# A two-layer hybrid decoder trunk on one core: buffers moved by 32 bytes, another place for one split block, and new orders at the ends of the output passes

## The chip, the cores and the metric

The kernel runs on one core of one Trainium2 chip. The metric is device time in microseconds (us) of that core, lower is better. The span of a profile runs from the first to the last instruction.

## The reference, cut to what matters

x is (1024 positions, 1024 channels), all float32. Each of two layers computes

```
h = rmsnorm(x) * (1 + scale) + shift          # scale, shift, gate from c_act @ mod_w[layer]
layer 0: proj = h @ hy_w_in   (1024 x 6144)    # six parts of 8 heads, 128 channels each
         ya = rg_lru(conv4(xa)) * silu(ga);  yb = gb_post * conv3(gc_pre * v) * silu(gb)
layer 1: proj = h @ pool_w_in (1024 x 4096)    # values v and gates g
         y = ((window_mean(v) - v) @ w_grp + b) * scale * silu(g)      # four groups of 512
x = x + gate * (y @ w_out)                     # w_out is 2048 x 1024
```

and the result is one more rmsnorm of x, times `final_g`.

## The kernel before, in words

**Precision.** Every large product is made of float32 operands split into an upper part (fp32r, by ScalarE) and a remainder (VectorE), and three matmuls: upper*upper, upper*lower, lower*upper (L2113, L2114, L2115 in `products`). Most are 128 x 128 weights against 512 columns.

**Order.** Every engine has its program written out by hand, with semaphores between them. Layer 0 goes head by head (Strassen-like pairs of products for heads 1 to 7), and spills each head's two blocks of y to DRAM. Then come the *passes*: pass A of layer 0 makes output blocks 0 to 2 (128 positions each), B makes 3 to 5, C makes 6 and 7; pass A of layer 1 makes 0 to 3 and B makes 4 to 7. A pass has 16 steps, one for each block of 128 channels of y. A step needs its rows of `w_out` (`split_hi` L865 on ScalarE, `split_lo` L1369 on VectorE) and its block of y (`split_y`, L932 and L1436). Three steps are held at a time, so both splits of step n wait until TensorE has counted step n-3 done (`o_step`, set at the last block's second half). A block has two halves of 512 columns, each with a bank of PSUM. All but the last `LAST` steps (2, in pass B of layer 1 it is 3) go step by step through the pass's blocks; the last ones go block by block: for each block, for each of these steps, both halves (L2462 to L2467). So blocks are complete one after the other.

**y's places.** The split y blocks of layer 0 lie in a ring of three: `y_at_r` over head buffer 0, `y_at_aux` over `aux`, and `y_at_xc` over head buffer 2 (XC, later SIGB), which is read last by `gate_b(7)` (L1675). In layer 1 they lie inside X. X, `w_hi`, `w_lo` and `raw` stand ahead of the small vectors in SBUF, all head buffers, the pooled differences `d_hi` and `d_lo` and layer 0's y behind them and behind `pad_small`, of 32 bytes. X begins at byte 640 of its partition and `w_hi` at byte 115,328, multiples of 64; the head buffers begin at 163,488, and everything behind them at an offset from there that is a multiple of 64 (`d_hi` at 180,128).

**After a block.** `residual` (L1811, L1815) multiplies each half by the gate and adds it to the rows of x. `squares` (L1167, L1170) makes the sum of squares of the row and its root, `inverse` (L1821) the reciprocal. In layer 0, `normalize` (L1175) scales the row, and TensorE transposes it back (`turn`, L2248: three groups of eight, woven behind steps by the table BEHIND, L147 to L150), ScalarE modulates (`modulate`, L1184 to L1194) and VectorE takes the lower part (`low_h1`). In layer 1, `row_out` (L1826) scales the row by its inverse and `final`, and SyncE stores it (`store`, L682).

**Ends.** After pass C, VectorE splits V0 and V1, does `low_h1(1, 7)`, and then `gate_of_layer_1` (L1842), which TensorE waits for before it goes on. At the kernel's end VectorE does, for each of blocks 4 to 7, `residual(1, b)` and `row_out(b)` (L2105 to L2107).

Of the kernel before, what the change touches and what calls it, by code (L numbers as in the profile page):

```python
# [109 lines left out]
def build(nc, x, c, norm_g, mod_w, mod_b, hy_w_in, hy_conv_w, hy_conv_b, lru_w_a, lru_b_a, lru_w_x, lru_b_x,  # L110
# [36 lines left out]
    BEHIND = {(0, "B", 5): ["mod1"], (0, "C", 13): ["gate1"]}  # L147
    for k in range(KB):
        BEHIND.setdefault((0, "B", 6 + k), []).append(("T", 0, k))
        BEHIND.setdefault((0, "C", 5 + k), []).append(("T", 1, k))  # L150

    def outputs(layer, p):

# [66 lines left out]
    with ExitStack() as ctx:  # L220
        def sb(name, shape, dt=F32, stack=ctx):
            return stack.enter_context(nc.sbuf_tensor(name, shape, dt))

        def sem(name):
            return ctx.enter_context(nc.semaphore(name))
# [24 lines left out]
        pos = sb("pos", [P, PAD], mybir.dt.int32)  # L250
        icnt = sb("icnt", [P, GROUPS, PAD])
        fix = sb("fix", [P, PAD])
        sb("pad_small", [P, PAD // 2])


        with ExitStack() as phase:
# [19 lines left out]
        with ExitStack() as phase:  # L276
            y_at_r = sb("y_at_r", [P, S], F32R, phase)
            sb("pad_r", [P, S], F32, phase)
            y_at_xc = sb("y_at_xc", [P, S], F32R, phase)
            xc_hi_ = sb("xc_hi_", [P, S], F32R, phase)  # L280
            xc_lo_ = sb("xc_lo_", [P, S], F32R, phase)
            sb("pad_heads", [P, 9, S], F32, phase)
            y_at_aux = sb("y_at_aux", [P, S], F32R, phase)
        with ExitStack() as phase:
            sb("pad_pool", [P, 4, PAD + S], F32, phase)
# [5 lines left out]
        def halves(ap):  # L291
            return ap.rearrange("p (a b) -> p a b", a=2)
# [45 lines left out]

        def y_half(n, which):

            return halves((y_at_r, y_at_aux, y_at_xc)[n][:, :])[:, which, :]


        def piece(at, width, dt=F32):
# [122 lines left out]
        mixed_done = sem("mixed_done")  # L467
        pads = sem("pads")
        row_ready = sem("row_ready")

        def v(name, n=0, count=1):
            return vec[:, COL[name] + n:COL[name] + n + count]
# [80 lines left out]
        def _(sp):  # L553
# [228 lines left out]
            for n, step in enumerate(s for s in STEPS if s[0] == 1):  # L782
# [11 lines left out]
                    sp.dma_start(final, final_g.rearrange("(a n) -> a n", a=1).broadcast_to([P, D])).then_inc(gate_in, 16)  # L794
                if p == "B" and at in (5, 7, 9, 11):
                    store((at - 5) // 2)
            for b in range(4, SB):
                store(b)
            sp.wait_ge(out_done, 16 * SB)

        LAM_STEPS = 3
        CONSTS = 6
# [55 lines left out]
        def _(act):  # L858
# [58 lines left out]
            def take_21(q):  # L917
                act.wait_ge(full_of["4"], q + 1)
                nc.scalar.activation(dst(q)[1][:, S1], bank(q, "a"), ACT.Copy, scale=-1.0).then_inc(neg21, 1)
# [234 lines left out]
                prep(cc, 6)  # L1154
            split_hi(("W", 0, "A", TIME_ORDER[1]))
            take_21(Q["C", HEADS - 1])
            sigmoid_b(HEADS - 1)
            split_hi(("W", 0, "A", TIME_ORDER[2]))
            act.wait_ge(sgb_done, HEADS)
            split_y((0, "A", TIME_ORDER[2]))  # L1160


            def squares(layer, b):
# [33 lines left out]
            def passes(layer, begin):  # L1197
                for n, step in enumerate(s for s in STEPS if s[0] == layer):
                    if n < begin:
                        continue  # L1200
                    p, at = "ABC"[n // 16], n % 16
                    step_splits(step)
                    if (p, at) == ("A", 15):
                        load_root()
                    if layer == 0:
                        if p == "B" and at in (2, 3, 4):
                            squares(0, at - 2)
                        if p == "B" and at in (3, 4, 5):
                            normalize(at - 3)
                        if p == "B" and at >= 9:  # L1210
                            modulate(0, at - 9)
                        if (p, at) == ("C", 0):
                            modulate(0, 7)
                        if p == "C" and at in (3, 4, 5):
                            squares(0, at)
                        if p == "C" and at in (4, 5, 6):
                            normalize(at - 1)
                        if p == "C" and at >= 8:
                            modulate(1, at - 8)
                    elif p == "B" and at in (3, 4, 5, 6):  # L1220
                        squares(1, at - 3)

# [127 lines left out]
            step_splits(first[1])  # L1350

            passes(1, 2)
            for b in range(4, SB):
                squares(1, b)

        @block.vector
        def _(dve):
# [315 lines left out]
            def gate_b(i):  # L1673
                dve.wait_ge(sgb_ready, i + 1)
                nc.vector.tensor_tensor(SGB, SGB, SIGB if i else area(("gb", 0)), ALU.mult).then_inc(sgb_done, 1)  # L1675
# [103 lines left out]
                inputs_of_scan(i)  # L1779
            recur(HEADS - 1)  # L1780
            split_lo(("W",) + first[1])
            gate_b(HEADS - 1)
            out_a(HEADS - 1)
            step_splits(first[2])
            out_b(HEADS - 1)


# [35 lines left out]
            def row_out(b):  # L1823
                inverse(1, b)
                dve.wait_ge(rstd_ready, SB + b + 1)
                nc.vector.scalar_tensor_tensor(out=XN[1][b], in0=XR[1][b], scalar=rstd[:, 2, b:b + 1], in1=final,  # L1826
                                               op0=ALU.mult, op1=ALU.mult).then_inc(row_ready, 1)

            def modulation_1():
                dve.wait_ge(*full("mod1"))  # L1830
# [30 lines left out]
            def passes(layer, begin):  # L1861
                for n, y_step in enumerate(s for s in STEPS if s[0] == layer):
                    p, at = "ABC"[n // 16], n % 16
                    if n >= begin:
                        if layer == 0 and p == "B":
                            if at == 1:
                                residual(0, 0)
                                residual(0, 1)
                            if at == 2:
                                residual(0, 2)  # L1870
                        if layer == 0 and p == "C":
                            if at == 1:
                                residual(0, 3)
                                residual(0, 4)
                            if at == 2:
                                residual(0, 5)
                        if layer == 1 and p == "B":
                            if at == 1:
                                residual(1, 0)
                                residual(1, 1)  # L1880
                                residual(1, 2)
                            if at == 2:
                                residual(1, 3)
                        step_splits(y_step)
                    if layer == 0:
                        for m in MODS_AT.get(n, ()):
                            add_mod(mods1[m])
                        if p == "B" and at in (2, 3, 4):
                            inverse(0, at - 2)
                        if (p, at) == ("B", 8):  # L1890
                            modulation_1()
                        if p == "B" and at >= 10:
                            low_h1(0, at - 10)
                        if p == "C" and at < 2:
                            low_h1(0, at + 6)
                        if p == "C" and at in (3, 4, 5):
                            inverse(0, at)
                        if (p, at) == ("C", 7):
                            window_counts()
                        if p == "C" and at >= 9:  # L1900
                            low_h1(1, at - 9)
                    elif p == "B" and at in (4, 5, 6, 7):
                        row_out(at - 4)

            passes(0, 3)
            split_lo(("V0", 0))
            split_lo(("V1", 0))
            low_h1(1, KB - 1)
            gate_of_layer_1()
            residual(0, 6)  # L1910
            inverse(0, 6)
# [190 lines left out]
            mixed(n, 3)  # L2102

            passes(1, 2)
            for b in range(4, SB):  # L2105
                residual(1, b)
                row_out(b)  # L2107

        @block.tensor
        def _(pe):  # L2110
# [340 lines left out]
            for layer, p in BLOCKS:  # L2451
                y_steps, blocks = [s for s in STEPS if s[:2] == (layer, p)], BLOCKS[layer, p]
                ends = 2 * KB - LAST[layer, p]
                for n, y_step in enumerate(y_steps[:ends]):
                    operands(y_step)
                    for b in blocks:
                        for half in range(2):
                            if (layer, p, n, b, half) == (0, "A", 0, 2, 1):
                                last_of(Q["C", HEADS - 1])
                            part_of(y_step, b, half)  # L2460
                    behind(layer, p, n)
                for b in blocks:  # L2462
                    for y_step in y_steps[ends:]:
                        if b == blocks[0]:
                            operands(y_step)
                        for half in range(2):
                            part_of(y_step, b, half)  # L2467
                for n in range(ends, 2 * KB):
                    behind(layer, p, n)
                if (layer, p) == (0, "C"):  # L2470
                    groups()
# [22 lines left out]
```

## Time and profile before

| | |
|---|---|
| three runs | 1337.77, 1338.64, 1338.72 us; median 1338.64 |
| the profiled execution | 1339.64 us, its span 1337.9 us |
| PE (matmul) | 1292.0 us busy, 97%, 5671 instructions |
| DVE (VectorE) | 936.2 us, 70%, 1122 |
| ACT (ScalarE) | 629.3 us, 47%, 885 |
| POOL | 271.4 us, 20%, 158 |
| granted TensorE clock | 0.982 of full speed |
| HBM read, written | 145.33 MB, 25.17 MB |

The profiled execution is 1.00 us above the median. Matmuls overlap their neighbours, so a row's duration (0.39 us) is longer than the distance from one start to the next; the distance is what counts. "[2.30 <-DVE ...]" behind a row is the engine's idle time before it and what ended it.

### The profile page before, as it was taken

The numbers are of one execution on the slowest core, as the hardware profiler recorded it, in microseconds if no ns is written. First come the engines' busy times: TensorE is split into PE (matmuls) and PEld (weight loads), VectorE is DVE, ScalarE is ACT, GpSimd is POOL, SyncE is SP. The second block draws the span as 40 slices with busy tenths as digits, with TensorE's granted clock in tenths as the row PEclk, the third lists the DMA queues.
The fourth block names the chain that finished last, engine by engine and source line by source line (L and its number), as shares of the span: only waits on it lengthen the run. The fifth ranks groups of instructions, "written<-read, shape, count | busy, mean of one in ns | idle before, by whom it ended". The sixth has DMA issues, their size and how long they took to land.

```text
span 1337.9 us, 15397 instructions
## 1 busy us (share of the span) xinstructions
PE 1292.0 (97%) x5671; PEld 1057.4 (79%) x5671; DVE 936.2 (70%) x1122; ACT 629.3 (47%) x885; POOL 271.4 (20%) x158
## 2 busy tenths in 40 slices
PE   4999999999999999999999999999999999999995
PEld 4877788888888888788877777888888888888884
DVE  6889887978878886767466597758658656435635
ACT  6465556564646465445467464243243143223422
POOL 0034433433534432000000022133133131000000
PEclk7899999999999999999899999999999999999998
DMA  9612241323232342597666202321320321873531
GB/s 297 196 49 67 63 130 55 123 83 110 67 110 85 93 130 79 198 380 266 231 200 221 79 16 64 101 88 32 110 79 33 110 79 41 300 247 128 215 108 63
DMA packets 145474, 171.51 MB, mean 128 GB/s; under 512 B 6582, under 2 KB 117366, under 8 KB 145400
## 3 DMA queue, kind: packets, MB, share of 16 engines
q1 hardware_dynamic: 145400, 170.53, 39.5%
q8 instruction: 46, 0.75, 0.2%
q14 instruction: 28, 0.23, 0.1%
HBM read 145.33 MB, written 25.17 MB: 127 GB/s over the span
## 4 chain that ended last, share of the span: by engine, by line
PE 82%; DVE 12%; issue 2%; ACT 2%; DMA 1%; SPq 0%; DVEq 0%; ACTq 0%
PE psum L2113 27%; PE psum L2115 27%; PE psum L2114 27%; DVE w_lo L1369 1%; DVE X L1459 1%; DVE win L1951 1%; DVE whole_x L1811 1%; DVE w_lo L1391 1%; DMA whole_x<-in_x 1%; DVE w_lo L1383 1%; DVE X L1465 1%; PE psum L2248 0%; ACT w_hi L865 0%; DVE d_lo L1969 0%; DMA raw<-in_hy_w_out 0%
## 5 line engine op out<-in xcount | busy, mean ns | idle before, releaser
L2113 PE MATMUL psum<-X,w_hi 128*128 128x512 f32 x1140 | 448.9, 394 | 9.9 <-DVE late L1842 2.8
L2115 PE MATMUL psum<-X,w_lo 128*128 128x512 f32 x1140 | 446.4, 392 | 0.0
L2114 PE MATMUL psum<-X,w_hi 128*128 128x512 f32 x1140 | 446.0, 391 | 0.0
L2113 PEld LDWEIGHTS psum<-X,w_hi 128*128 128x128 f32 x1140 | 215.5, 189 | 60.3 <-issue 9.1
L2115 PEld LDWEIGHTS psum<-X,w_lo 128*128 128x128 f32 x1140 | 215.2, 189 | 45.5
L2114 PEld LDWEIGHTS psum<-X,w_hi 128*128 128x128 f32 x1140 | 215.5, 189 | 44.7 <-issue 0.2
L1369 DVE TENSOR_TENSOR w_lo<-raw,w_hi 128x1024 fp32r<-128x1024 f32 x98 | 120.9, 1235 | 166.1 <-ACT w_hi L865 165.8
L865 ACT ACTIVATE w_hi<-raw 128x1024 fp32r<-128x1024 f32 x98 | 103.6, 1058 | 211.6 <-PE psum L2115 171.9
L887 ACT ACTIVATE w_hi<-ssum 128x512 fp32r<-128x512 f32 x140 | 87.2, 626 | 121.0 <-PE psum L2115 95.4
L1391 DVE TENSOR_TENSOR w_lo<-ssum,w_hi 128x512 fp32r<-128x512 f32 x140 | 119.1, 857 | 27.4 <-ACT w_hi L887 26.7
L826 POOL TENSOR_TENSOR ssum<-raw 128x512 f32<-128x512 f32 x35 | 62.0, 1772 | 302.4 <-DMA raw<-in_pool_w_in 266.2
L834 POOL TENSOR_TENSOR ssum<-ssum,raw 128x512 f32<-128x512 f32 x35 | 55.8, 1593 | 323.7 <-DVE w_lo L1391 323.7
L2113 PE MATMUL psum<-w_hi,X 128*128 128x512 f32 x256 | 99.8, 390 | 0.4 <-DVE X L1436 0.4
L2115 PE MATMUL psum<-w_hi,X 128*128 128x512 f32 x256 | 99.6, 389 | 0.0
L2114 PE MATMUL psum<-w_lo,X 128*128 128x512 f32 x256 | 99.6, 389 | 0.0
L837 POOL TENSOR_TENSOR ssum<-raw 128x512 f32<-128x512 f32 x35 | 78.2, 2234 | 73.4 <-DVE w_lo L1391 73.4
L831 POOL TENSOR_TENSOR ssum<-ssum,raw 128x512 f32<-128x512 f32 x35 | 61.5, 1759 | 49.3 <-DVE w_lo L1391 47.3
L1383 DVE TENSOR_TENSOR w_lo<-raw,w_hi 128x1024 fp32r<-128x1024 f32 x35 | 42.7, 1221 | 27.1 <-ACT w_hi L876 26.9
L2113 PEld LDWEIGHTS psum<-w_hi,X 128*128 128x128 f32 x256 | 48.0, 188 | 11.0 <-DVE w_lo L1369 0.8
L2115 PEld LDWEIGHTS psum<-w_hi,X 128*128 128x128 f32 x256 | 48.0, 188 | 10.1
L2114 PEld LDWEIGHTS psum<-w_lo,X 128*128 128x128 f32 x256 | 48.1, 188 | 9.9
L2113 PE MATMUL psum<-d_hi,w_hi 128*128 128x512 f32 x128 | 50.7, 396 | 0.3 <-DVE w_lo L1369 0.3
(239 smaller groups left out, 1959.4 us busy)
## 6 DMA issues: line engine op xcount, KB each, us to landing
raw<-in_hy_w_in SPq DMA_DIRECT2D x48, 512.0 KB, 5.1
raw<-in_hy_w_out SPq DMA_DIRECT2D x48, 512.0 KB, 4.7
raw<-in_pool_w_in SPq DMA_DIRECT2D x32, 512.0 KB, 5.2
raw<-in_pool_w_out SPq DMA_DIRECT2D x32, 512.0 KB, 3.6
aux<-in_mod_w SPq DMA_DIRECT2D x16, 512.0 KB, 4.2
y_dram<-bufs SPq DMA_DIRECT2D x16, 512.0 KB, 2.9
raw<-in_mod_w SPq DMA_DIRECT2D x16, 512.0 KB, 5.6
y_dram<-gb_ SPq DMA_DIRECT2D x16, 512.0 KB, 3.1
```

Source lines behind the costliest of these rows:

```text
L826: nc.gpsimd.tensor_tensor(even, a21, a22, ALU.add).then_inc(s_ready, 1)
L831: nc.gpsimd.tensor_tensor(odd, even, a11, ALU.add).then_inc(s_ready, 1)
L834: nc.gpsimd.tensor_tensor(even, odd, a12, ALU.add).then_inc(s_ready, 1)
L837: nc.gpsimd.tensor_tensor(odd, a21, a11, ALU.add).then_inc(s_ready, 1)
L865: nc.scalar.activation(flat(w_hi[:, es:es + 2, :]), raw[:, at, :], ACT.Copy).then_inc(hi_done, 1)
L887: nc.scalar.activation(w_hi[:, es, :], ssum[:, op % 2, :], ACT.Copy).then_inc(hi_done, 1)
L1369: nc.vector.tensor_tensor(flat(w_lo[:, es:es + 2, :]), raw[:, at, :], flat(w_hi[:, es:es + 2, :]).bitcast(F32), ALU.subtract).then_inc(lo_ ...
L1383: ins = nc.vector.tensor_tensor(w_lo[:, es:es + 2, :].rearrange("p two (k n) -> p two k n", k=KP), raw_blocks(q, 0), w_hi[:, es:es + 2, :] ...
L1391: ins = nc.vector.tensor_tensor(w_lo[:, es, :], ssum[:, op % 2, :], w_hi[:, es, :].bitcast(F32), ALU.subtract)
L2113: nc.tensor.matmul(out_, whi, xhi, start=first, stop=False, skip_group_check=check)
L2114: nc.tensor.matmul(out_, whi, xlo, start=False, stop=False, skip_group_check=check)
L2115: return nc.tensor.matmul(out_, wlo, xhi, start=False, stop=last, skip_group_check=check)
```

## The change

Five things. (1) `pad_small` goes, so all buffers behind it begin 32 bytes lower (the head buffers at 163,456). (2) The third place of y's ring lies over head buffer 8 (GBP) instead of buffer 2; GBP is last read by `gated_sc(7)`. The splits of step 2 of pass A move ahead of `sigmoid_b(7)` on ScalarE and ahead of `gate_b(7)` on VectorE, where `out_a(7)` moves ahead too. (3) The last steps of each pass go half by half: block, then half, then step. (4) The second group of transposes goes behind steps 4 to 11 of pass C instead of 5 to 12, with `modulate` and `low_h1` a step earlier. (5) At the end, VectorE does `residual(1, b+1)` ahead of `row_out(b)`; the last block has its squares, its scaled row and its store in halves.

```diff
-        BEHIND.setdefault((0, "C", 5 + k), []).append(("T", 1, k))
+        BEHIND.setdefault((0, "C", 4 + k), []).append(("T", 1, k))
...
-        sb("pad_small", [P, PAD // 2])
...
-            y_at_xc = sb("y_at_xc", [P, S], F32R, phase)
+            sb("pad_xc", [P, S], F32, phase)
...
+            y_at_gbp = sb("y_at_gbp", [P, S], F32R, phase)
...
-            for b in range(4, SB):
+            for b in range(4, SB - 1):
                 store(b)
-            sp.wait_ge(out_done, 16 * SB)
+            for half, cols in enumerate(HALVES):
+                sp.wait_ge(row_ready, SB + half)
+                sp.dma_start(out[0, (SB - 1) * P:SB * P, cols], XN[1][SB - 1][:, cols]).then_inc(out_done, 16)
+            sp.wait_ge(out_done, 16 * (SB + 1))
...  (ScalarE)
+            act.wait_ge(scg_done, HEADS)
+            split_y((0, "A", TIME_ORDER[2]))
+            split_hi(("W", 0, "A", TIME_ORDER[2]))
             sigmoid_b(HEADS - 1)
-            split_hi(("W", 0, "A", TIME_ORDER[2]))
-            act.wait_ge(sgb_done, HEADS)
-            split_y((0, "A", TIME_ORDER[2]))
...
-                        if p == "C" and at >= 8:
-                            modulate(1, at - 8)
+                        if p == "C" and 7 <= at < 15:
+                            modulate(1, at - 7)
...
+            b = SB - 1
+            for half, cols in enumerate(HALVES):
+                act.wait_ge(o_evac, o_count(1, b, half))
+                nc.scalar.activation(XN[1][b][:, cols], XR[1][b][:, cols], ACT.Square,
+                                     accum_out=ss[:, 2 * half, b:b + 1]).then_inc(sq_done, 1)
+                act.wait_ge(sq_done, 2 * SB + half)
+                if half == 0:
+                    nc.scalar.activation(ss[:, 1, b:b + 1], ss[:, 0, b:b + 1], ACT.Identity, scale=1.0 / D,
+                                         bias=cst[:, 0:1]).then_inc(half_done, 1)
+                    act.wait_ge(half_done, 1)
+                else:
+                    nc.scalar.activation(sd[:, 2, b:b + 1], ss[:, 2, b:b + 1], ACT.Sqrt, scale=1.0 / D,
+                                         bias=ss[:, 1, b:b + 1]).then_inc(root_done, 1)
...  (VectorE)
+            out_a(HEADS - 1)
+            split_y(first[2])
+            split_lo(("W",) + first[2])
             gate_b(HEADS - 1)
-            out_a(HEADS - 1)
-            step_splits(first[2])
             out_b(HEADS - 1)
...
-                        if p == "C" and at >= 9:
-                            low_h1(1, at - 9)
+                        if p == "C" and at >= 8:
+                            low_h1(1, at - 8)
...
-            low_h1(1, KB - 1)
             gate_of_layer_1()
...
-            for b in range(4, SB):
-                residual(1, b)
-                row_out(b)
+            residual(1, 4)
+            residual(1, 5)
+            row_out(4)
+            residual(1, 6)
+            row_out(5)
+            residual(1, 7)
+            row_out(6)
+            last_row_out()     # inverse, then the scaled row in two halves, row_ready after each
...  (TensorE)
                 for b in blocks:
-                    for y_step in y_steps[ends:]:
-                        if b == blocks[0]:
-                            operands(y_step)
-                        for half in range(2):
+                    for half in range(2):
+                        for y_step in y_steps[ends:]:
+                            if (b, half) == (blocks[0], 0):
+                                operands(y_step)
                             part_of(y_step, b, half)
```

## Rows read from the trace of the kernel before

**Rows 1.** The page's chain that ended last, by engine.
```profile
PE 82%; DVE 12%; issue 2%; ACT 2%; DMA 1%; SPq 0%; DVEq 0%; ACTq 0%
```
**Rows 2.** Timeline, PE, layer 0 pass A: start us, us; 53 distances between these.
```profile
582.09 0.40 PE L2113 MATMUL psum<-w_hi,y_at_r 128*128 128x512 f32 x1
...
594.46 0.40 PE L2115 MATMUL psum<-w_hi,y_at_xc 128*128 128x512 f32 x1
```
**Rows 3.** Timeline, PE, layer 1 pass A into B: 402 distances between these.
```profile
1150.49 0.40 PE L2113 MATMUL psum<-w_hi,X 128*128 128x512 f32 x1
...
1241.63 0.45 PE L2113 MATMUL psum<-w_hi,X 128*128 128x512 f32 x1
```
**Rows 4.** Timeline, PE, mixing of group 0: 71 distances between these.
```profile
854.02 0.40 PE L2113 MATMUL psum<-d_hi,w_hi 128*128 128x512 f32 x1
...
870.59 0.40 PE L2115 MATMUL psum<-d_hi,w_lo 128*128 128x512 f32 x1
```
**Rows 5.** Timeline, PE, a gate product of six matmuls, then the next product.
```profile
209.38 0.39 PE L2113 MATMUL psum<-xc_hi_,g_hi 128*128 128x512 f32 x1
...
210.76 0.39 PE L2113 MATMUL psum<-X,w_hi 128*128 128x512 f32 x1
```
**Rows 6.** Groups by form, ACT, squares: name, count | busy, mean ns | idle.
```profile
L1167 ACT ACTIVATE whole_x<-whole_x 128x1024 f32<-128x1024 f32 x8 | 8.4, 1053 | 17.9 <-DVE whole_x L1815 17.9
L1167 ACT ACTIVATE whole_x<-bufs 128x1024 f32<-128x1024 f32 x8 | 8.4, 1049 | 7.2 <-DVE bufs L1815 7.2
```
**Rows 7.** Timeline, the start of layer 0's pass A.
```profile
544.75 0.60 ACT L919 ACTIVATE bufs<-psum 128x512 f32<-128x512 f32 x1 [5.66 <-PE psum L2115]
...
547.79 1.23 DVE L1675 TENSOR_TENSOR bufs<-bufs 128x1024 f32<-128x1024 f32 x1 [3.47 <-ACT bufs L1064]
...
551.90 0.47 PE L2113 MATMUL psum<-w_hi,y_at_xc 128*128 128x512 f32 x1 [2.30 <-DVE y_at_xc L1436]
...
552.92 0.33 SPq L635 DMA_DIRECT2D y_dram<-bufs  x1
...
561.01 0.47 PE L2113 MATMUL psum<-w_hi,y_at_aux 128*128 128x512 f32 x1 [0.47 <-DVE y_at_aux L1436]
```
**Rows 8.** Timeline, layer 0, pass B's end and pass C's first steps.
```profile
686.91 1.06 ACT L865 ACTIVATE w_hi<-raw 128x1024 fp32r<-128x1024 f32 x1 [4.83 <-PE psum L2115]
...
694.31 0.48 PE L2113 MATMUL psum<-w_hi,y_at_aux 128*128 128x512 f32 x1 [0.49 <-DVE y_at_aux L1436]
...
702.51 1.14 ACT L1175 ACTIVATE whole_x<-bufs,rstd 128x1024 f32<-128x1024 f32 x1
...
705.60 0.49 PE L2248 MATMUL psum<-ident,whole_x 128*128 128x128 f32 x3
```
**Rows 9.** Timeline, the end of pass C and the first matmul behind it.
```profile
736.78 1.06 ACT L865 ACTIVATE w_hi<-raw 128x1024 fp32r<-128x1024 f32 x1 [4.85 <-PE psum L2115]
...
740.87 0.50 PE L2113 MATMUL psum<-X,w_hi 128*128 128x512 f32 x1 [2.79 <-DVE late L1842]
```
**Rows 10.** Timeline, ACT, layer 1, the split for step 1 of pass B.
```profile
1235.77 1.06 ACT L865 ACTIVATE w_hi<-raw 128x1024 fp32r<-128x1024 f32 x1 [7.94 <-PE psum L2115]
```
**Rows 11.** Timeline, layer 1, the last splits and blocks of pass B.
```profile
1307.95 1.06 ACT L865 ACTIVATE w_hi<-raw 128x1024 fp32r<-128x1024 f32 x1 [3.86 <-PE psum L2115]
...
1311.02 0.47 PE L2113 MATMUL psum<-w_hi,X 128*128 128x512 f32 x1 [0.45 <-DVE X L1436]
...
1329.04 0.68 DVE L1811 TENSOR_TENSOR whole_x<-psum,whole_x 128x512 f32<-128x512 f32 x1
...
1331.82 1.06 ACT L1167 ACTIVATE whole_x<-whole_x 128x1024 f32<-128x1024 f32 x1 [4.20 <-DVE whole_x L1815]
...
1333.52 1.28 DVE L1826 SCALAR_TENSOR_TENSOR whole_x<-whole_x,rstd 128x1024 f32<-128x1024 f32 x1
```
**Rows 12.** DMA view of 1300 to 1338 us: GB/s in 40 slices of 0.95 us.
```profile
GB/s 0 0 0 0 0 0 0 0 0 9 0 0 0 0 0 0 0 0 0 177 358 17 17 0 0 177 375 0 0 0 0 190 362 0 0 0 0 198 354 0
```
**Rows 13.** Windows: length, PE, PEld, DVE, ACT, POOL busy (count), PEclk, DMA share, GB/s.
```profile
740.00:744.00 4.00, 3.13 (x8) 2.47 (x9) 3.41 (x6) 0.49 (x1) 0.00 (x0) 0.67 0.00 1
```

More of the change, by code:

```diff
@@ L278, in build @@
             sb("pad_r", [P, S], F32, phase)
-            y_at_xc = sb("y_at_xc", [P, S], F32R, phase)
+            sb("pad_xc", [P, S], F32, phase)
             xc_hi_ = sb("xc_hi_", [P, S], F32R, phase)
             xc_lo_ = sb("xc_lo_", [P, S], F32R, phase)
-            sb("pad_heads", [P, 9, S], F32, phase)
+            sb("pad_heads", [P, 3, S], F32, phase)
+            y_at_gbp = sb("y_at_gbp", [P, S], F32R, phase)
+            sb("pad_late", [P, 5, S], F32, phase)
             y_at_aux = sb("y_at_aux", [P, S], F32R, phase)
@@ L339, in y_half @@
         def y_half(n, which):
-            return halves((y_at_r, y_at_aux, y_at_xc)[n][:, :])[:, which, :]
+            return halves((y_at_r, y_at_aux, y_at_gbp)[n][:, :])[:, which, :]
         def piece(at, width, dt=F32):
@@ L469, in build @@
         row_ready = sem("row_ready")
+        half_done = sem("half_done")
         def v(name, n=0, count=1):
@@ L1352, in _ @@
             passes(1, 2)
-            for b in range(4, SB):
+            for b in range(4, SB - 1):
                 squares(1, b)
+            b = SB - 1
[11 more added lines that the diff above has]
+                                         bias=ss[:, 1, b:b + 1]).then_inc(root_done, 1)
         @block.vector
@@ L1827, in row_out, with last_row_out @@
                                                op0=ALU.mult, op1=ALU.mult).then_inc(row_ready, 1)
+            def last_row_out():
+                b = SB - 1
+                inverse(1, b)
+                dve.wait_ge(rstd_ready, 2 * SB)
+                for cols in HALVES:
+                    nc.vector.scalar_tensor_tensor(out=XN[1][b][:, cols], in0=XR[1][b][:, cols],
+                                                   scalar=rstd[:, 2, b:b + 1], in1=final[:, cols],
+                                                   op0=ALU.mult, op1=ALU.mult).then_inc(row_ready, 1)
             def modulation_1():
@@ L2104, in _ @@
             passes(1, 2)
-            for b in range(4, SB):
-                residual(1, b)
-                row_out(b)
+            residual(1, 4)
[6 more added lines that the diff above has]
+            last_row_out()
         @block.tensor
```

## The prediction

> **What bounds the kernel now.** I read the chain that ended last first: TensorE is 82% of it, VectorE 12% [rows 1]. So a change pays where it shortens TensorE's row of matmuls, takes away a wait in it, or shortens what stands behind its last matmul. Next I read the distance between matmul starts in undisturbed stretches, since almost the whole span is such distances. Layer 1's y products take (1241.63 - 1150.49) / 402 = 226.7 ns each [rows 3]; layer 0's, the same instruction with its weights in the head buffers, 12.37 / 53 = 233.4 ns [rows 2]; mixing, where the columns streamed (d_hi) lie there, 16.57 / 71 = 233.4 ns [rows 4]. A gate product, both of whose operands lie there, takes 1.38 / 6 = 230 ns [rows 5]. Third come the waits: 2.30 and 0.47 us at steps 2 and 4 of pass A [rows 7], 0.49 at step 2 of pass C [rows 8], 2.79 at the end of pass C [rows 9], 0.45 in the last pass [rows 11]. Last comes the tail: matmuls end near 1324.7, the span at 1337.9.
>
> **Part 1, the start of buffers.** What the slow stretches share is an operand at 32 past a multiple of 64 bytes. The extra 6.6 ns is the same whether the weights (512 bytes a partition) or the columns (2048 bytes) begin there, as one more read of a 64-byte piece per operand would give: 16 float32 elements against 512 in 213 ns is 6.7 ns. I take 226.7 for all of them; bounds are 233.4 (no effect) and 226.7. Matmuls touched: 3 x 256 = 768 of layer 0's y, 4 x 96 = 384 of mixing, 96 of the gates at 3 ns. Whole: 768 x 6.6 = 5.1, 384 x 6.6 = 2.5, 0.3: 7.9 us. ScalarE's squares take 1053 ns in X and 1049 in the head buffers [rows 6], so I count nothing for the other engines and DMAs (bounds 0 to 1 us of gain).
> Not all of it arrives. Where a VectorE or ScalarE chain sets when TensorE may go on, its matmuls ahead are covered: 72 between step 13 of pass A and step 2 of B, and about 60 at B's end and C's start. Arriving: 0.3 and 0.1 ahead of the waits, pass A steps 4 to 13 180 x 6.6 = 1.2, B 252 x 6.6 = 1.6, C 129 x 6.6 = 0.85, mixing 2.5: **6.6 us**.
> On this the Trainium skill (SBUF — State Buffer, the table of properties) says that SBUF has cachelines of 16 bytes. A start at 32 past 64 is a whole line then, and by that rule the term would be 0. The trace's 233.4 against 226.7 speaks for a coarser piece.
>
> **Part 2, the third place of y.** Now sigmoid_b, gate_b (547.79), out_a and two splits stand ahead of 551.90 [rows 7]. In the new order y's upper part follows the copy at 544.75, so from 545.4; w's upper part to 546.8, w's lower to 548.1, ahead of the 549.4 at which TensorE asks: the 2.3 us go. Then the next thing is late. Behind the split stand a table load (1.28) and the sigmoid to 549.2, gate_b, out_b to 551.6; the last spill, now at 552.92, goes at 551.6, 1.3 earlier, and the loads for step 4 are queued behind it on SyncE. So step 4 starts at about 559.7 in place of 561.01, with a wait of some 2 us ahead of it: **1.3 us** gained of 2.8. If the DMA queues, busy from there on, set the pace alone, it is 0; if they carry the earlier start fully, 2.3.
>
> **Part 3, half by half.** The step before the last is now counted done 3 matmuls (0.7 us) before the pass's end, not 6, so the first split for the next pass starts 0.7 later.
> - A to B: VectorE is in residuals until 612.6 and hides it. 0.
> - B to C: ScalarE's split moves from 686.91 [rows 8] 0.7 later against TensorE, VectorE's chain behind it (w, y, low_h1, four residual operations, w, y) has no gap, and step 2 waits **0.7** longer.
> - C to layer 1: VectorE's chain from ScalarE's 736.78 to 740.87 [rows 9] starts 0.7 later and loses low_h1(1, 7), 0.53: **-0.15**.
> - Pass A to B of layer 1: the chain from 1235.77 [rows 10] ends in residual(1, 3), whose second half frees the bank that 1241.63 [rows 3] just waited for: **-0.4**.
> - Last pass: three steps at the end. The third's operands are asked for after 6 matmuls, not 12, but come no sooner (released at 1307.95, ready at 1311.02 [rows 11]). The wait grows by 6 x 0.227 = 1.36 and TensorE ends 1.36 later. In the tail's sum below.
>
> **Part 4, transposes a step earlier.** The first now stands behind step 4 of C, whose end falls near 702.8; it needs normalize(5), which is ScalarE's 702.51 to 703.65 [rows 8], in a queue without a gap since 691. With step 2 later, TensorE waits some **0.5** more here (bounds 0, if ScalarE's queue slides ahead, and 1.0). B to C and this cost 1.2 together.
>
> **Part 5, the tail.** Now each of the last blocks costs VectorE a round trip: residual 1329.04 to squares 1331.82 (2.78), to the scaled row 1333.52 (1.70), row end 1334.80 [rows 11], 5.7 us a block against TensorE's 4.08 (18 x 0.227). Turned round, with the same durations: TensorE starts the third step's first half at 1311.02, block 7's halves are full at 1324.25 and 1326.3. VectorE takes them at 1325.0 and 1326.3 and ends 1327.7; first half's squares on ScalarE end 1327.1, the second's run 1327.7 to 1328.5, root 1328.8. VectorE meanwhile writes row 6 (to 1329.1), then the reciprocal and two half rows to 1329.9 and 1330.5, in place of 1334.80. Then 1 MB is under way at once: at 198 to 375 GB/s a slice [rows 12] 512 KB takes some 1.45 us, so from 1329.9 the three stores run to 1332.8, plus the 0.85 that the last slice lies ahead of the end now: 1333.7 against 1337.9, **4.2 us** gained. Bounds: 2.5 (half rows of 2 KB store more slowly), 4.8 (the last store lands unqueued).
>
> **Sum.** 6.6 + 1.3 - 1.2 - 0.15 - 0.4 + 4.2 = 10.3 us. Against the profiled execution's 1339.64 that is 1329.3; the median of the runs shown lies 1.0 lower, so **1328.3**.
>
> **Rivals.**
> - *The start does not matter, only the region* (0.10). For it: all slow operands lie behind byte 163,000, and the 16-byte lines of the skill's SBUF page would have it so. Against: with both operands there the distance is 230, not more. It gives 10.3 - 6.6 = 3.7 gained: 1334.9.
> - *The granted clock falls at a longer wait* (0.12). Behind the wait of 2.79 the clock was 0.67 of full over 4 us, 1.2 GHz for a part, and PE did 8 matmuls in place of 17 or so [rows 13]; behind the one of 2.30 it did not fall. New waits of about 2 us stand ahead of step 4 of A, in C and in the last pass. Price about 2 us each where nothing hides it: 1330.3 to 1332.3.
> - *The end is set by stores* (0.05). Two half stores and row 6 share the queues and the halves land late: tail gain 1.5 at most, 1331.0.
> - *Slower: the ring of transposes* (0.03). A transpose waits for modulate two before it, which is in ScalarE's queue behind a split that waits for TensorE. If the shift closes this ring, each of 8 steps of C grows. It decides from 1.3 us a step, 10.4 in all: 1339 or more. Against: before and after, each stands the same distance in steps from the other, and no such wait shows now.
> - That the change doesn't do what it says is not open for places and orders; for the pace it is the first rival.
>
> **Numbers.** The forecast itself has 0.66, with its own range 1326.0 to 1330.8 (the bounds of parts 2, 4 and 5); 0.04 is left for more gain than that, from DMAs or waits that shorten by themselves. 8 in 10: 1325.5 to 1333.0, which takes in the clock and the stores, and leaves out the first rival and the slower one. A measurement of this kernel can tell about 0.2%, 2.7 us, from nothing. Faster by more 0.91 (the first rival is 3.7 faster), within 0.05, slower 0.04.
>
> **What the profile after would show.** Distances of 226.7 ns between matmuls with y_at_* and d_hi; 233 would make the forecast wrong by 6 us. No wait at y_at_gbp's first use, one of about 2 us at step 4 of pass A. Longer waits at step 2 of C and at its first transpose. About 1.8 us of wait in the last pass, the last matmul 1.4 later against step 12, the last half row some 4 us after the last matmul's end, and the span's end 3 us behind that. A PEclk below 1.00 near 557, 694 or 1311 would be the second rival.

## The result, and the profile after

The changed kernel takes 1327.18 us in the median of five runs (1323.81 to 1330.55), the kernel before 1337.77 beside it (1336.99 to 1338.72). The ratio is 0.9923, with a 95% interval of 0.9902 to 0.9945. The prediction was 1328.3 us. The profiled execution took 1326.77 us, its span 1325.0, which is 12.9 us below the span before; the medians lie 10.6 us apart. All ratios are of fast executions: one of steps_back's six runs took 3335.56 us, nothing is known of why, and its ratio leaves that run out.

The page after, first its busy time, then the chain that ended last:

```profile
PE 1281.4 (97%) x5671; PEld 1054.8 (80%) x5671; DVE 936.2 (71%) x1123; ACT 629.6 (48%) x888; POOL 271.3 (20%) x158
...
PE 81%; DVE 13%; issue 2%; ACT 2%; DMA 1%; SPq 0%; DVEq 0%; ACTq 0%
```

The picture is that of [rows 1]: TensorE's row of matmuls sets the end. The same number of matmuls is 10.6 us less busy (1292.0 before).

The pace, that is the distance from one matmul's start to the next, by TensorE's timeline: 109 undisturbed distances between layer 0's y matmuls, then 71 in mixing.

```profile
575.07 0.39 PE L2147 MATMUL psum<-w_lo,y_at_gbp 128*128 128x512 f32 x1
...
599.77 0.39 PE L2148 MATMUL psum<-w_hi,y_at_gbp 128*128 128x512 f32 x1
...
847.63 0.39 PE L2146 MATMUL psum<-d_hi,w_hi 128*128 128x512 f32 x1
...
863.72 0.39 PE L2148 MATMUL psum<-d_hi,w_lo 128*128 128x512 f32 x1
```

24.70 / 109 = 226.6 ns where [rows 2] had 233.4, and 16.09 / 71 = 226.6 where [rows 4] had 233.4. Over all such distances y's mean is 227.5 to 227.7 (233.3 before), a gate product's 226.7 (229.9 before).

TensorE's waits, by its timeline, in brackets with the releaser:

```profile
555.68 0.47 PE L2146 MATMUL psum<-w_hi,y_at_aux 128*128 128x512 f32 x1 [2.01 <-DVE y_at_aux L1455]
...
687.65 0.47 PE L2146 MATMUL psum<-w_hi,y_at_aux 128*128 128x512 f32 x1 [1.37 <-DVE y_at_aux L1455]
...
696.88 0.55 PE L2281 MATMUL psum<-ident,whole_x 128*128 128x128 f32 x3 [0.78 <-ACT whole_x L1180]
...
734.66 0.58 PE L2146 MATMUL psum<-X,w_hi 128*128 128x512 f32 x1 [2.97 <-DVE late L1871]
...
1233.07 0.50 PE L2146 MATMUL psum<-w_hi,X 128*128 128x512 f32 x1 [0.29 <-DVE whole_x L1835]
...
1302.51 0.47 PE L2146 MATMUL psum<-w_hi,X 128*128 128x512 f32 x1 [1.80 <-DVE X L1455]
```

Step 2 of pass A waits no more. Step 4 waits 2.01 (0.47 in [rows 7]), step 2 of C 1.37 (0.49 in [rows 8]), the first transpose 0.78 (none), the end of C 2.97 (2.79 in [rows 9]), the last pass 1.80 (0.45 in [rows 11]).

The tail, VectorE's and TensorE's timeline, which answers to [rows 11]:

```profile
1316.40 0.68 DVE L1831 TENSOR_TENSOR whole_x<-psum,whole_x 128x512 f32<-128x512 f32 x1
...
1317.33 0.39 PE L2148 MATMUL psum<-w_hi,X 128*128 128x512 f32 x1
...
1319.28 1.28 DVE L1846 SCALAR_TENSOR_TENSOR whole_x<-whole_x,rstd 128x1024 f32<-128x1024 f32 x1
1320.48 0.15 DVE L1841 RECIPROCAL rstd<-sd 128x1 f32<-128x1 f32 x1
1320.67 1.42 DVE L1854 SCALAR_TENSOR_TENSOR whole_x<-whole_x,rstd 128x512 f32<-128x512 f32 x2
```

Block 7's residual begins ahead of the last matmul's start, at 1316.40; it began 4.5 us behind it before (1329.04 against 1324.51). The half rows end at 1322.1, the span 2.9 us later. From the last matmul's start to the end are 7.67 us, 13.39 before.

**How traces are compared below.** Some stretches run at half the clock, 1.2 GHz, and they differ between executions of one kernel. A product's matmul takes 0.427 us there instead of 0.227, so I count those at a distance of 0.36 to 0.45 us and take 0.2 us off for each (one or two in a profile can be counted wrongly): "row less clock" is the start of the last matmul, less the start of the first product near 35 us, less 0.2 us for each product's matmul at half clock. It leaves out what half clock costs the small matmuls. The most of that lies in layer 0's 32 column sums near 635 us, so the table has the time that these take, too.

| kernel | first product | last matmul | at half clock | row less clock | column sums | last matmul to end |
|---|---|---|---|---|---|---|
| before | 35.83 | 1324.51 | 38 | 1281.1 | 4.74 | 13.39 |
| tail_only | 34.38 | 1322.52 | 42 | 1279.7 | 3.63 | 8.28 |
| place_only | 35.70 | 1323.38 | 45 | 1278.7 | 3.63 | 13.32 |
| start_only | 35.88 | 1313.69 | 24 | 1273.0 | 3.63 | 13.31 |
| heads_256 | 35.72 | 1314.96 | 30 | 1273.2 | 3.63 | 13.34 |
| start_64 | 35.69 | 1319.83 | 29 | 1278.3 | 3.63 | 13.37 |
| heads_128 | 34.61 | 1319.19 | 35 | 1277.6 | 4.77 | 13.31 |
| changed kernel | 35.18 | 1317.33 | 26 | 1277.0 | 4.66 | 7.67 |
| after_again (same) | 35.68 | 1321.93 | 46 | 1277.1 | 3.96 | 7.67 |
| turns_back | 35.84 | 1319.83 | 40 | 1276.0 | 4.62 | 7.67 |
| steps_back | 35.83 | 1314.70 | 21 | 1274.7 | 4.43 | 8.30 |
| steps_again (same) | 35.38 | 1313.97 | 24 | 1273.8 | 4.13 | 8.33 |
| both_back | 34.66 | 1315.40 | 40 | 1272.7 | 3.83 | 8.30 |
| late_half | 35.30 | 1313.44 | 19 | 1274.3 | 4.48 | 7.66 |

Equal rows of matmuls agree in row less clock to 0.1 us (changed kernel and after_again), 0.9 (steps_back and steps_again) and 1.4 (before and tail_only). Of the 1.4, the column sums are 1.11. Their row in before's timeline of TensorE, then the windows of before and of tail_only around it (columns as in [rows 13]):

```profile
636.71 4.74 PE L2254 MATMUL psum<-ones,bufs 128*128 128x1 f32 x32
```

```profile
636.00:648.00 12.00, 12.00 (x58) 10.48 (x57) 3.98 (x7) 3.04 (x5) 0.00 (x0) 0.72 0.85 304
```

```profile
636.00:648.00 12.00, 12.00 (x65) 10.28 (x64) 4.61 (x7) 4.98 (x8) 0.00 (x0) 0.86 0.92 338
```

The granted clock was 0.72 of full speed there in before and 0.86 in tail_only. So kernels with equal column sums are compared best. What is smaller than that is read from single waits, which agree to some 0.02 us where the releaser is a chain of VectorE's.

### The profile page after: what moved, and what is told of

Its sections match the earlier page's. It is cut to its first block, busy times and chain, and to the rows that moved or that the text cites. A ratio compares the mean times of both kernels' runs of the same rounds, so it can differ in the third digit from the quotient of the medians.

```text
span 1325.0 us, 15403 instructions
## 1 busy us (share of the span) xinstructions
PE 1281.4 (97%) x5671; PEld 1054.8 (80%) x5671; DVE 936.2 (71%) x1123; ACT 629.6 (48%) x888; POOL 271.3 (20%) x158
## 4 chain that ended last, share of the span: by engine, by line
PE 81%; DVE 13%; issue 2%; ACT 2%; DMA 1%; SPq 0%; DVEq 0%; ACTq 0%
PE psum L2146 27%; PE psum L2147 26%; PE psum L2148 26%; DVE w_lo L1388 1%; DVE X L1478 1%; DVE win L1979 1%; ACT w_hi L870 1%; DVE whole_x L1831 1%; DVE w_lo L1410 1%; DMA whole_x<-in_x 1%; PE psum L2281 1%; DVE w_lo L1402 1%; DVE X L1484 1%; DVE d_lo L1997 0%; DVE macc L1503 0%
```

## The experiments

**One part alone.** Three kernels put one part of the change into the kernel before.

start_only, the start of the buffers:

```
-        sb("pad_small", [P, PAD // 2])
```

> Nothing but the start of the buffers changes. Theory of the prediction (an operand that begins 32 bytes past a multiple of 64 costs each matmul 6.6 ns): layer 0's y matmuls 226.7 to 227.7 ns apart in place of 233.4, mixing 226.7, gate products 226.7 in place of 230; the waits at steps 2 and 4 of pass A, at step 2 of C and at the end of C as before; 6.6 us less than before, 1331.2. Rival (only the region counts, not the start): 233.4 ns as before, the time within 1 us of before's. If the scanning and splitting engines also gain: more than 7.9 us less.

Measured: 1328.37 us, ratio 0.9940 (0.9925 to 0.9955), 8.0 us of 1337.1. TensorE's timeline of start_only, 109 distances in layer 0 and 71 in mixing:

```profile
572.01 0.39 PE L2113 MATMUL psum<-w_lo,y_at_aux 128*128 128x512 f32 x1
...
596.71 0.39 PE L2114 MATMUL psum<-w_hi,y_at_aux 128*128 128x512 f32 x1
...
845.86 0.39 PE L2112 MATMUL psum<-d_hi,w_hi 128*128 128x512 f32 x1
...
861.95 0.39 PE L2114 MATMUL psum<-d_hi,w_lo 128*128 128x512 f32 x1
```

24.70 / 109 and 16.09 / 71 are 226.6 ns; y's mean is 227.5 to 227.7, gate products 226.7. The waits at step 2 of pass A (2.44) and at the end of C (2.83) are nearly as before. The others are not, against the expectation: step 2 of C waits 0.78 in place of 0.49, a wait of 0.28 is new at step 2 of B, and step 4 of pass A doesn't wait, as six matmuls ran at half clock ahead of it. Row less clock is 1273.0; tail_only, whose column sums took the same 3.63 us and whose row of matmuls is before's, has 1279.7: 6.7 us. The forecast had 6.6 arriving of 7.9; the interval of the runs, 6.0 to 10.0 us, holds both. The pace rests on the start, and the first rival falls.

tail_only, the order behind the last pass (residuals ahead of rows, halves for the last block):

> Before with nothing but the order behind the last pass: residuals ahead of the scaled rows, the last block's squares, scaled row and store by halves. The matmuls keep their old order, so TensorE ends as before and the last block's first half is full only 0.7 us ahead of its end. My theory (VectorE's round trips set the end): the last half row some 4 us after the last matmul, the stores 3 us more, 5.5 us less than before: 1332.3. Rival (stores set the end): half rows land late, at most 3 us less, 1334.8 or more. In either case nothing changes ahead of 1311 us.

Measured: 1332.85 us, ratio 0.9960 (0.9945 to 0.9976). The last matmul to the end takes 8.28 in place of 13.39: 5.1 us, near my 5.5 and not the rival's 3. By the ratio of the runs it is 5.3 us (3.2 to 7.4).

place_only, y's third place and the orders it allows:

> Before with nothing but y's third buffer in another place and the orders that this allows. My theory: the wait of 2.30 us at step 2 of pass A goes, and one of about 2 us stands at step 4 (0.47 before), as the loads behind the last spill come no more than 1.3 us earlier: 1.3 us less than before, 1336.5. Rival 1 (the loads carry it fully): 2.3 less and 0.5 us of wait at step 4. Rival 2 (DMA queues pace it): 0 less, a wait of 2.8 at step 4; a clock below full behind it would add 1 to 2 us.

Measured: 1335.78 us, ratio 0.9989 (0.9978 to 1.0000), so 1.5 us with 0 in its interval: the runs alone can't tell it from nothing. TensorE's timeline of place_only, step 4 of pass A:

```profile
559.69 0.47 PE L2116 MATMUL psum<-w_hi,y_at_aux 128*128 128x512 f32 x1 [1.87 <-DVE y_at_aux L1438]
```

No wait at step 2, and 1.87 at step 4, which starts at 559.69 against the 561.01 of [rows 7]: 1.3 us, as forecast. Eight matmuls behind this wait ran at half clock, so its 1.3 could be lost again in this execution.

**Where a buffer should begin.** The start alone tells that 32 bytes matter, not which piece. start_64 makes the gap 64 bytes in place of 32 (PAD is 16 elements of 4 bytes):

```
-        sb("pad_small", [P, PAD // 2])
+        sb("pad_small", [P, PAD])
```

> Before with the 32 bytes ahead of the big buffers made 64: they begin at an odd multiple of 64 bytes, where in the changed kernel they begin at a multiple of 512. If the piece that an operand should begin with is 64 bytes, the same as with the start alone: 226.7 ns and 6.6 us less, 1331.2. If it is 128 bytes or more, 233.4 ns and before's time, 1337.8.

Measured: 1336.31 us, ratio 0.9991 (0.9983 to 0.9999). TensorE's timeline of start_64, 54 distances in layer 0 and 71 in mixing:

```profile
583.24 0.39 PE L2113 MATMUL psum<-w_hi,y_at_r 128*128 128x512 f32 x1
...
595.84 0.39 PE L2113 MATMUL psum<-w_hi,y_at_r 128*128 128x512 f32 x1
...
850.76 0.40 PE L2113 MATMUL psum<-d_hi,w_hi 128*128 128x512 f32 x1
...
867.03 0.39 PE L2115 MATMUL psum<-d_hi,w_lo 128*128 128x512 f32 x1
```

12.60 / 54 = 233.3 ns for y, as slow as with 32 bytes, and 16.27 / 71 = 229.2 for mixing, between the two paces. So the piece is not 64 bytes. A gap of 128 bytes ahead of the whole region (start_128) gave no time: SBUF has 16,352 bytes a partition left for a buffer of 16,384. The next two start from start_only and move only the buffers in the heads' region, y's among them, by 128 and by 256 bytes; mixing's stay:

```
+            sb("pad_bufs", [P, 32], F32, phase)      # 64 in heads_256
             bufs = sb("bufs", [P, 12, S], F32, phase)
...  (the same ahead of xT and of y_at_r, which begin at the same byte)
```

> The kernel with the start alone, and 128 bytes ahead of y's buffers and of those that share their place (mixing's stay where they are, at 256 past a multiple of 512). With y 32 or 64 bytes past a multiple of 128 its matmuls stood 233.4 ns apart, at a multiple of 512 they stand 227.6. If the piece is 128 bytes: 227.6 here. If it is 256 or 512 bytes: 233.4. Mixing 226.7 in either case.

> As the kernel with y's buffers 128 bytes further, but 256 bytes: y begins at 256 past a multiple of 512, as mixing's streamed columns do in the kernel with the start alone, which stand 226.7 ns apart. If the piece that matters is 256 bytes: y's matmuls 227.6 ns apart and the time of the kernel with the start alone, 1328.4. If it is 512 bytes for the weights: 233.4 ns and 1334 as with 128 bytes. If y is slow from the shift of its neighbours and not from its own start: 233.4 ns too, at 128 and at 256 alike.

heads_128 took 1334.31 us (one run, so it has no interval), heads_256 1330.11, ratio 0.9952 (0.9936 to 0.9969). TensorE's timeline of heads_128, 106 distances in layer 0, and of heads_256, 109:

```profile
575.20 0.39 PE L2116 MATMUL psum<-w_lo,y_at_aux 128*128 128x512 f32 x1
...
599.83 0.39 PE L2117 MATMUL psum<-w_hi,y_at_aux 128*128 128x512 f32 x1
```

```profile
575.22 0.39 PE L2116 MATMUL psum<-w_lo,y_at_aux 128*128 128x512 f32 x1
...
599.93 0.39 PE L2117 MATMUL psum<-w_hi,y_at_aux 128*128 128x512 f32 x1
```

24.63 / 106 = 232.4 ns and 24.71 / 109 = 226.7. heads_128's pace is that of the expectation's case of 256 or 512 bytes, but for 1 ns, and heads_256 decides for 256. The expectations count the starts from X and leave out the 640 bytes ahead of it. By true byte addresses, modulo 256 (X and `w_hi` begin at 128 in all):

| kernel | y begins at | y, mean ns | d_hi begins at | mixing, mean ns | gate products, mean ns |
|---|---|---|---|---|---|
| before | 163,488, 160 | 233.3 | 160 | 233.4 | 229.9 |
| start_64 | 163,520, 192 | 233.3 | 192 | 229.2 | 230.5 |
| heads_128 | 163,584, 0 | 232.4 | 128 | 226.7 | 228.2 |
| start_only, changed kernel | 163,456, 128 | 227.6 | 128 | 226.7 | 226.7 |
| heads_256 | 163,712, 128 | 227.6 | 128 | 226.7 | 226.7 |

Of four starts tried, one is fast: 128 past a multiple of 256, which is where X and `w_hi` begin. A start at a multiple of 256 itself is slow when the other operand begins at 128. Whether what counts is that place or that both operands begin alike is open: moving X and `w_hi` as well wasn't tried. The gate products, whose operands both lie in the heads' region and move together, speak against "alike" as the whole rule (229.9 and 228.2 at 160 and 0).

**One part undone.** steps_back leaves the half-by-half order to the very last block:

```
-                    for half in range(2):
-                        for y_step in y_steps[ends:]:
+                    by_half = (layer, p, b) == (1, "B", blocks[-1])
+                    steps = y_steps[ends:]
+                    order = ([(y, half) for half in range(2) for y in steps] if by_half else
+                             [(y, half) for y in steps for half in range(2)])
...
```

> The changed kernel with only the very last block of the last pass ended half by half; every other block ends step by step, as before the change. My theory (a pass that ends half by half asks for the next step's operands 0.7 us sooner in layer 0 and 1.4 us sooner in the last pass, and they come no sooner): the wait in the last pass is 0.45 us in place of 1.80, the one at step 2 of pass C some 0.5 to 0.7 shorter than its 1.37, the 0.29 ahead of the last pass gone; the last matmul to the end of the span stays 7.7 us. 2.3 us less than the changed kernel: 1324.9 against its 1327.2. Rival: the longer waits come from part 1's faster matmuls alone, not from the order; then nothing changes, 1327.2.

Measured: 1325.82 us, ratio 0.9908 (0.9887 to 0.9930), which the runs can't tell from the changed kernel's 0.9923. TensorE's timeline of steps_back:

```profile
688.77 0.47 PE L2146 MATMUL psum<-w_hi,y_at_aux 128*128 128x512 f32 x1 [0.77 <-DVE y_at_aux L1455]
...
697.99 0.55 PE L2281 MATMUL psum<-ident,whole_x 128*128 128x128 f32 x3 [0.78 <-ACT whole_x L1180]
...
735.10 0.50 PE L2146 MATMUL psum<-X,w_hi 128*128 128x512 f32 x1 [2.30 <-DVE late L1871]
...
1301.23 0.47 PE L2146 MATMUL psum<-w_hi,X 128*128 128x512 f32 x1 [0.44 <-DVE X L1455]
```

Step 2 of C waits 0.60 less, the end of C 0.67 less, the last pass 1.36 less, and the 0.29 ahead of it is gone: 2.9 us, as the order explains and the pace doesn't. But the last matmul to the end grew from 7.67 to 8.30, against my "stays": the halves did buy something in the tail.

turns_back puts the second group of transposes, `modulate` and `low_h1` a step later again (`4 + k` to `5 + k`):

> The changed kernel with the second group's transposes, and the work that follows them, one step later again, as before. My theory: the wait of 0.78 us at the first transpose goes, and the wait at the end of pass C (2.97) grows by up to 0.53, as low_h1's last piece is back ahead of the gate: between 0.8 less and equal, 1326.4 to 1327.2. Rival (the earlier transposes paid for themselves by more than their wait): 1 us or more slower than the changed kernel.

Measured: 1328.30 us, ratio 0.9926 (0.9907 to 0.9946), the same as the changed kernel by the runs. `low_h1(1, 7)` stands ahead of the gate again. TensorE's timeline of turns_back:

```profile
690.60 0.47 PE L2147 MATMUL psum<-w_hi,y_at_aux 128*128 128x512 f32 x1 [1.37 <-DVE y_at_aux L1455]
...
737.15 0.50 PE L2147 MATMUL psum<-X,w_hi 128*128 128x512 f32 x1 [3.51 <-DVE late L1871]
```

No wait at the first transpose (0.78 gone), and 3.51 at the end of C, 0.54 more. So part 4 costs 0.78 and brings 0.54.

both_back has the edits of steps_back and of turns_back together:

> The two edits together. If the two costs add up: 2.5 us less than the changed kernel, 1324.7. If they are the same wait (step 2 of C only moves it to the first transpose), no less than with the steps alone.

Measured: 1325.63 us, ratio 0.9911 (0.9891 to 0.9931). The waits are 0.78 at step 2 of C, none at the transpose, 2.83 at the end of C: the two costs add up. By the waits that is 0.25 us less than steps_back (0.78 less, 0.53 more), which the runs can't tell.

**What the halves are worth, and a better kernel.** In the last pass the third of the last three steps asks for its operands in the first block only. late_half keeps that block step by step and does the other three half by half; all other passes go step by step. Beside it ran the changed kernel once more (after_again) and the kernel of steps_back once more (steps_again):

```
+                    by_half = (layer, p) == (1, "B") and b != blocks[0]
```

> The last pass's first block step by step, its other three half by half; all other passes step by step. Theory: VectorE works without a gap through the tail and starts block 5's first half 1.3 us earlier, of which 0.6 arrive (its second half is full at the same time): the last matmul to the end 7.7 us in place of 8.3, and the third step's operands are still asked for after 12 matmuls, so that the wait stays 0.44: 0.6 less than the kernel with steps, 2.3 to 2.5 less than the changed kernel. Rival: the end is set by ScalarE's roots and the stores, 8.3 stays.

> The changed kernel once more, beside the next two on one chip: 1327.2 in the median of its runs before. What it is to tell is whether the stretches at half the clock, behind the waits near 36, 135, 557, 634 and 735 us, differ from run to run of the same kernel. Theory: each such matmul costs 0.2 us, their number differs (26 in the profiled run before), and the span less 0.2 us for each is the same within 1 us: 1325.0 - 5.0 = 1320.0.

> The changed kernel with only the very last block ended half by half, again: last matmul to the end of the span 8.3 us, 0.44 us of wait in the last pass, and the span less the half clock's matmuls 1.7 to 1.9 us less than the changed kernel's: 1318.2. If the earlier gain was a matter of the clock alone, no less than the changed kernel's 1320.0.

The three ran beside each other, before at 1335.98: after_again 1329.49, ratio 0.9944 (0.9929 to 0.9958); steps_again 1324.77, 0.9907 (0.9893 to 0.9922); **late_half 1323.17, 0.9900 (0.9884 to 0.9917)**. Both are clear of after_again's interval; the two can't be told from each other by the runs. TensorE's and VectorE's timeline of late_half:

```profile
1299.95 0.47 PE L2146 MATMUL psum<-w_hi,X 128*128 128x512 f32 x1 [0.44 <-DVE X L1455]
...
1303.67 0.69 DVE L1831 TENSOR_TENSOR whole_x<-psum,whole_x 128x512 f32<-128x512 f32 x1
1304.39 0.69 DVE L1835 TENSOR_TENSOR whole_x<-whole_x 128x512 f32<-128x512 f32 x1
1305.71 0.69 DVE L1831 TENSOR_TENSOR whole_x<-psum,whole_x 128x512 f32<-128x512 f32 x1 [0.62 <-PE psum L2148]
...
1313.44 0.39 PE L2148 MATMUL psum<-w_hi,X 128*128 128x512 f32 x1
```

VectorE of steps_back, the same place:

```profile
1306.29 0.69 DVE L1831 TENSOR_TENSOR whole_x<-psum,whole_x 128x512 f32<-128x512 f32 x1 [1.35 <-PE psum L2148]
```

VectorE has block 5's first half 9.77 us ahead of the last matmul's start (1303.67 to 1313.44), in steps_back 8.41 (1306.29 to 1314.70). In both, VectorE works without a gap to its end from there, but for 0.62 us in late_half at 1305.71, where the second half is full no sooner. So of the 1.36 us 0.64 arrive: 7.66 us to the end in place of 8.30, with the wait still 0.44. late_half takes both.

By row less clock, with equal tails, late_half is 2.7 us shorter than the changed kernel (1277.0 - 1274.3), where 2.3 to 2.5 were expected; steps_again's span less clock is 1322.3 - 4.8 = 1317.5 (1318.2 expected). The runs show more, 0.9900 against 0.9944, some 5.9 us. In the profiles the rest is the clock: late_half has 19 matmuls at half clock, after_again 46, 5.4 us of the 8.5 between their spans (1321.1 and 1329.6). Windows of the changed kernel and of after_again, the same program (length, PE, PEld, DVE, ACT and POOL busy, PEclk, DMA share, GB/s), one fence for each:

```profile
36.00:44.00 8.00, 8.00 (x34) 6.54 (x34) 5.65 (x13) 3.36 (x4) 0.00 (x0) 0.84 0.55 158
136.00:140.00 4.00, 4.00 (x19) 3.28 (x18) 3.96 (x4) 1.69 (x4) 2.27 (x1) 1.00 0.05 20
```

```profile
36.00:44.00 8.00, 8.00 (x30) 6.48 (x30) 5.02 (x12) 2.72 (x3) 0.00 (x0) 0.71 0.47 133
136.00:140.00 4.00, 3.66 (x10) 2.92 (x11) 3.80 (x5) 1.96 (x4) 2.24 (x2) 0.57 0.31 119
```

In the second row of each, behind the same wait of 2.14 and 2.17 us, one execution does 19 matmuls in 4 us and the other 10. after_again had 46 at half clock and a span of 1329.6, the changed kernel 26 and 1325.0: 20 x 0.2 = 4.0 of the 4.6 us between them, and 0.5 more lie ahead of the first product. That part of its expectation holds: 1329.6 - 9.2 = 1320.4 against 1319.8.

## Why the prediction was right

**The sum.** Forecast 1329.3 for a profiled execution, measured 1326.77, 2.5 us less. The profile before had 38 matmuls at half clock, the one after 26: 12 x 0.2 = 2.4 us, which no step of the prediction claims. TensorE's first product also lay 0.65 us earlier, in a stretch that the change doesn't touch. Without the two, 9.8 of the 12.9 us are left against a sum of 10.3. So the sum was of the right size. The median forecast, 1328.3, was met by 1327.18.

**Part 1, 6.6 us.** The distances came out as forecast (226.6 in the rows shown, 227.6 in y's mean), and start_only, with nothing else changed, gains 6.7 us in row less clock against tail_only and 8.0 by the runs (6.0 to 10.0). heads_256, with its column sums at 3.63 us as well, gains 6.5. So 6.6 of 7.9 arriving was right, as far as the traces tell. **The reason given was wrong.** I had "an operand at 32 past a multiple of 64 bytes" and one more read of a 64-byte piece; starts at a multiple of 64 (start_64) and of 128 bytes (heads_128) are slow as well. That was luck: 32 bytes down led to the one fast place in four. The Trainium skill (SBUF — State Buffer, Specifications (TRN2)) has cachelines of 16 bytes, and by that rule the term was to be 0: all starts tried are multiples of 32, and their paces differ by 6.6 ns, so the measurement decides against it as a rule for this. The other engines behave as forecast, no faster (VectorE 936.2 us busy before and after, ScalarE 629.3 and 629.6).

**Part 2, 1.3 us.** Right in each step: the wait at step 2 is gone, that at step 4 is 2.01 ("some 2 us"). From ScalarE's copy (544.75 in [rows 7], 540.73 now) to step 4 it is 14.95 us, 16.26 before: 1.31 less. The reason holds, too. SyncE issues the first load behind the last spill 8.54 us after that copy before, 7.25 now, 1.29 less (its queue's timeline, before, then after):

```profile
553.29 0.85 SPq L586 DMA_DIRECT2D raw<-in_hy_w_out  x1
```

```profile
547.98 0.43 SPq L588 DMA_DIRECT2D raw<-in_hy_w_out  x1
```

From the copy to step 4 the profiles with the new place have 14.8 to 15.3 us (place_only 15.13), those with the old one 16.1 to 17.7.

**Part 3.** B to C was forecast at +0.7 on 0.49, so 1.2; it is 1.37, and undoing the order takes 0.60 away. The other 0.28 come with the pace, as a faster TensorE meets the same chain sooner (0.78 in steps_back and in start_only). The last pass was exact: +1.36 forecast, 1.80 against 0.45, and 1.36 less in steps_back. Pass A to B of layer 1: 0.29 of new wait for 0.4. C to layer 1: a cost of 0.15 forecast, 2.97 against 2.79, which is 0.18; undoing part 3 takes 0.67 away and undoing part 4 adds 0.54, the two terms of that step (0.7 and 0.53). What the prediction didn't set apart, as its tail sum has the halves' new times in it, is what the order brings: 0.63 us in the tail (8.30 to 7.67).

**Part 4, 0.5 us.** 0.78 at the first transpose, inside the bounds of 0 and 1.0. Together with B to C it is 1.66 in place of 1.2.

**Part 5, 4.2 us.** 13.39 - 7.67 = 5.72 behind the last matmul, less the 1.36 ahead of it: 4.4, where 4.2 was forecast. The terms fit too: the last half row was to be written 4.2 us behind the last full half (1330.5 against 1326.3), it is 4.4 behind the last matmul's end (1322.1 - 1317.7), and the stores took 2.9 us more, 3.2 forecast. VectorE's round trip was the bound, not the stores, so that rival falls.

**The clock rival** (0.12) did not come true in the execution profiled first: at 555.68 and 1302.51, behind 2.01 and 1.80 us, the clock did not fall. At step 4 of pass A it did fall in three of the eight profiles with the new place: place_only (behind 1.87 us), after_again (2.37) and both_back (2.10), for seven or eight matmuls. But the prediction's "behind the one of 2.30 it did not fall" is no rule: of the six profiles with the old place it fell behind the wait at step 2 in three, tail_only (2.30), start_only (2.44) and heads_128 (2.33), for six to nine. So the price is real, about 1.2 to 1.8 us a time; it comes in some executions and not in others, with the old place as with the new one.

**The slower rival**, a ring of transposes, would have shown as a wait at each of eight steps. There is one, at the first.

**What the change leaves.** Of parts 3 and 4, the half-by-half order costs 2.9 us of waits and brings 0.64 in the tail, and this 0.64 is to be had without them (late_half). The rest of the gain is the start, the place and the tail.

## What to carry to other kernels

Compare the distance between matmuls of the same shape over different operands: 6.6 ns in 233 looked like nothing and was the largest term, and it came from where a buffer begins. Test the start at several places before believing a piece size; the first theory that explains one shift may be wrong for the next.

An order that completes work sooner at the end of a stage also asks for its inputs sooner at the beginning of that end. Keep the old order in the block that asks, and use the new one only in those that are waited for.

Before taking a difference of two profiles as the change's, count the matmuls at half clock in both, the small ones too: here that is 4 to 9 us of one execution and differs by up to 4 between equal programs.

## What the runs showed that I had not expected

- **The fast start is 128 past a multiple of 256 bytes**, where TensorE's other operand begins too. At a multiple of 256 y's matmuls take 232.4 ns, at 160 and 192 past it 233.3, at 128 past it 227.6. Streamed columns (d_hi) at 192 take 229.2, less than the 233.4 at 160. The mechanism is open.
- **The clock behind a wait is not decided by the wait's length alone.** At the end of pass C the wait was 2.29 or 2.30 us in steps_back, steps_again and late_half, and none of the three had a matmul at half clock behind it. With waits of 2.79 to 3.51 us there, nine of eleven profiles had seven to nine, and two had none (start_only and heads_256, both at 2.83 us), though both_back waited the same 2.83 and had eight. A shorter wait there brought more than its own length: from its end to the wait near 793 the changed kernel takes 59.0 us (734.66 to 793.69), steps_back 57.8 (735.10 to 792.91).
- **A row of matmuls that is the same in two kernels moved by 1.4 us** between their profiles (before and tail_only) once the products at half clock were taken off. Most of it is the clock again: the 32 column sums near 637 us took 4.74 us in before and 3.63 in tail_only, and a count of the large matmuls alone misses that. For steps of 0.3 to 1.3 us, only single waits and their releasers decide.
